# First block: x loaded in two halves, late half turned behind the first products, second weight chunk in quarters, rotation tables and memory rows moved

## The reference

```python
h = rms_norm(x, norm_mix)
aq, ak, av, iq, ik, iw, bq, bk, bv = _split(h @ w_in, AB_SIZES)      # AB_WIDTH 2472
aq = partial_rope(rms_norm(aq.reshape(B, S, DSA_HEADS, HEAD_DIM), a_q_norm), positions)
ak = partial_rope(rms_norm(ak.reshape(B, S, 1, HEAD_DIM), a_k_norm), positions)[:, :, 0]
iq = partial_rope(iq.reshape(B, S, DSA_IDX_HEADS, DSA_IDX_DIM), positions)
o_a = dsa_attention(aq, ak, av, iq, ik, iw)       # top 64 keys by an index score
bq, bk = ...
o_b = moba_attention(bq, bk, bv)
x = x + concatenate([o_a, o_b]) @ w_out
```

## Time and profile before

| | us |
|---|---|
| median of 3 runs | 1660.42 |
| lowest, highest | 1660.26, 1661.79 |
| span of the profiled execution, from the first to the last instruction | 1659.6 |
| TensorE busy | 1619.1 (98%) |
| VectorE busy | 1096.3 (66%) |
| ScalarE busy | 891.3 (54%) |
| POOL busy | 421.5 (25%) |

### The profile page before, as it was taken

How to read it: one execution, slowest core, us unless ns; L and a number is a source line. 1 busy time by engine, 2 the same in 40 slices (tenths; PEclk the granted TensorE clock), 3 DMA queues, 4 the chain that set the end, 5 groups by cost and what they waited for, 6 DMA issues and landing times. The chain is left out here.

```text
span 1659.6 us, 26949 instructions
## 1 busy us (share of the span) xinstructions
PE 1619.1 (98%) x10929; PEld 1462.8 (88%) x10929; DVE 1096.3 (66%) x1546; ACT 891.3 (54%) x1401; POOL 421.5 (25%) x460
## 2 busy tenths in 40 slices
PE   8999999999999999999999999999999999999999
PEld 7767899987887889998889998999888999999997
DVE  6875665645576665655577768777646876867763
ACT  6465554434455555443456746566445684756652
POOL 2500100002341120000147802244204690214430
PEclk9999999999999999999999999999999999999999
DMA  7523376556330236665555444766556444376652
GB/s 278 174 77 101 103 205 194 185 197 213 99 135 27 77 102 172 185 186 193 174 195 164 147 133 147 189 185 190 181 154 220 159 153 130 131 204 187 190 179 76
DMA packets 287067, 265.30 MB, mean 160 GB/s; under 512 B 12256, under 2 KB 247520, under 8 KB 286944
## 3 DMA queue, kind: packets, MB, share of 16 engines
q1 hardware_dynamic: 286944, 263.59, 50.8%
HBM read 262.52 MB, written 1.05 MB: 159 GB/s over the span
## 5 line engine op out<-in xcount | busy, mean ns | idle before, releaser
L144 DVE TENSOR_TENSOR w_lo<-w_raw,w_hi 128x2048 fp32r<-128x2048 f32 (+2 forms) x244 | 565.8, 2321 | 288.6 <-ACT w_hi L143 283.6
L143 ACT ACTIVATE w_hi<-w_raw 128x2048 fp32r<-128x2048 f32 (+2 forms) x244 | 462.9, 1902 | 214.6 <-PE bank L529 125.5
L1873 PE MATMUL bank<-h_hi,w_hi 128*128 128x256 f32 x1984 | 565.5, 285 | 4.7 <-issue 1.2
L1874 PE MATMUL bank<-h_lo,w_hi 128*128 128x256 f32 x1984 | 561.3, 283 | 0.0
L1875 PE MATMUL bank<-h_hi,w_lo 128*128 128x256 f32 x1984 | 561.2, 283 | 0.0
L1873 PEld LDWEIGHTS bank<-h_hi,w_hi 128*128 128x128 f32 x1984 | 380.5, 192 | 8.2 <-issue 7.5
L1874 PEld LDWEIGHTS bank<-h_lo,w_hi 128*128 128x128 f32 x1984 | 380.7, 192 | 0.1
L1875 PEld LDWEIGHTS bank<-h_hi,w_lo 128*128 128x128 f32 x1984 | 380.6, 192 | 0.0
L456 PE MATMUL bank<-w_hi,h_hi 128*128 128x512 f32 (+1 forms) x288 | 113.4, 394 | 5.4 <-DVE w_lo L144 3.3
L2953 POOL TENSOR_TENSOR cffn_hidden<-cffn_conv 128x256 f32<-128x256 f32 x44 | 73.7, 1675 | 155.5 <-ACT cffn_conv L2984 155.5
L457 PE MATMUL bank<-w_lo,h_hi 128*128 128x512 f32 (+1 forms) x288 | 111.9, 388 | 0.0
(11 more groups left out here) (447 smaller groups left out, 2858.0 us busy)
## 6 DMA issues: line engine op xcount, KB each, us to landing
w_raw<-in_w_in SPq DMA_DIRECT2D x48, 1024.0 KB, 5.0
w_raw<-in_ffn_w_in SPq DMA_DIRECT2D x88, 512.0 KB, 5.0
w_raw<-in_w_up SPq DMA_DIRECT2D x88, 512.0 KB, 5.2
w_raw<-in_ffn_w_out SPq DMA_DIRECT2D x22, 1024.0 KB, 4.9
w_raw<-in_w_down SPq DMA_DIRECT2D x22, 1024.0 KB, 5.0
w_raw<-in_nsa_w_in SPq DMA_DIRECT2D x10, 1024.0 KB, 5.2
w_raw<-in_mem_w_kv SPq DMA_DIRECT2D x8, 1024.0 KB, 5.1
w_raw<-in_w_branch SPq DMA_DIRECT2D x8, 1024.0 KB, 5.1
```

Source lines behind the costliest of these rows:

```text
L143: return act.activation(hi, raw, ACT.Copy)
L144: return dve.tensor_tensor(self.lo[:, cut_slot, 0:k * n], raw, hi.bitcast(F32), ALU.subtract)
L1873: pe.matmul(out, h, hi[:, f, :], start=(f == 0), stop=False)
L1874: pe.matmul(out, h, lo[:, f, :], start=False, stop=False)
```

## The change

x comes in two DMAs of 512 columns each, with the gains, the positions and chunk 0's first half between them. TensorE turns the first half of the features before the first product, and the second half (`turn_late`) inside block 0, behind the six products of feature 0. Chunk 1 goes through `FirstChunk` as well: loaded in two halves, rounded and cut in four tiles. On ScalarE it is now rounded behind the squares and the table activations. On VectorE the 17 table instructions stand behind tile 1 of chunk 0. POOL fills the tables' inputs before it waits for the squares. The memory rows are loaded before chunk 3 and turned behind chunk 2, at (1, 0). The head gains are loaded last.

```diff
 class FirstChunk:
-    def __init__(self, k, chunk):
+    def __init__(self, k, chunk, c):
...
-        self.landed = [self.w.early_in[0], s("first_landed")]
-        self.rounded, self.cut = s("first_rounded"), s("first_cut")
+        self.landed = [self.w.early_in[c], s(f"first_landed{c}")]
+        self.rounded, self.cut = s(f"first_rounded{c}"), s(f"first_cut{c}")
...
 Project.pe
-                if c or self.tiles is None:
+                if c not in self.tiles:
                     w.wait_cut(pe, c)
...
+                    if j == 0 and ahead is not None:
+                        ahead(pe, f)
                     if j == 0:
                         self.features.wait_feature(pe, f)
-                    if c == 0 and self.tiles is not None:
-                        self.tiles.wait_cut(pe, k)
+                    if c in self.tiles:
+                        self.tiles[c].wait_cut(pe, k)
...
 block.sync
-                sp.dma_start(k.x[:, :, :], a["x"].rearrange("(t p) d -> p t d", p=P)).then_inc(x_in, 16)
+                x = a["x"].rearrange("(t p) d -> p t d", p=P)
+                sp.dma_start(k.x[:, :, 0:D // 2], x[:, :, 0:D // 2]).then_inc(x_in, 16)
                 sp.dma_start(k.gains_1[:, :], a["cols_1"]).then_inc(cols_in, 16)
+                rope_tables.load(sp)
+                first[0].load(sp, 0)
+                sp.dma_start(k.x[:, :, D // 2:D], x[:, :, D // 2:D]).then_inc(x_in_late, 16)
+                first[0].load(sp, 1)
                 for part in range(2):
-                    first.load(sp, part)
-                for c in range(1, w.EARLY):
-                    w.load(sp, w.chunks[c], w.raw_slot(c), w.early_in[c])
+                    first[1].load(sp, part)
+                w.load(sp, w.chunks[2], w.raw_slot(2), w.early_in[2])
+                mem.load(sp)
+                w.load(sp, w.chunks[3], w.raw_slot(3), w.early_in[3])
                 sp.dma_start(gain[:, :], row_bcast(a["rows"], 256)).then_inc(gains_in, 16)
-                rope_tables.load(sp)
-                mem.load(sp)
...
 block.gpsimd
+                rope_tables.pool(pool)
                 rows.factors(pool, 4)
-                rope_tables.pool(pool)
...
 block.scalar
-                for i in range(3):
+                for i in range(2):
                     rows.round(act, range(2 * i, 2 * i + 2))
-                    first.round(act, i)
-                first.round(act, 3)
+                    first[0].round(act, i)
+                rows.round(act, range(4, 6))
+                first[0].round(act, 2)
                 rows.round(act, range(6, KD))
-                w.round_to(act, 1)
+                first[0].round(act, 3)
                 for t in range(T):
                     for part in range(2):
+                        if part == 1:
+                            act.wait_ge(x_in_late, 16)
                         rows.square(act, t, part)
+                rope_tables.act(act)
+                for i in range(4):
+                    first[1].round(act, i)
                 w.round_to(act, 2)
-                rope_tables.act(act)
...
 block.vector
-                for i in range(3):
+                for i in range(2):
                     rows.cut(dve, range(2 * i, 2 * i + 2))
-                    first.split(dve, i)
-                first.split(dve, 3)
+                    first[0].split(dve, i)
+                rope_tables.dve(dve)
+                rows.cut(dve, range(4, 6))
+                first[0].split(dve, 2)
                 rows.cut(dve, range(6, KD))
-                w.cut_to(dve, 1)
-                rope_tables.dve(dve)
+                first[0].split(dve, 3)
+                for i in range(4):
+                    first[1].split(dve, i)
+                w.cut_to(dve, 2)
...
 block.tensor
                 pe.wait_ge(x_in, 16)
-                rows.turn_all(pe)
+                for t in range(T):
+                    rows.turn(pe, t, 0)
+
+                def turn_late(pe, f):
+                    if f == 1:
+                        pe.wait_ge(x_in_late, 16)
+                        for t in range(T):
+                            rows.turn(pe, t, 1)
...
-                    if (j, part) == (0, 1):
+                    if (j, part) == (1, 0):
                         mem.turn(pe)
...
-                project.pe(pe, index)
+                project.pe(pe, index, turn_late)
```

More of the change, by code:

```diff
@@ L207 @@
 class FirstChunk:
-    def __init__(self, k, chunk):
+    def __init__(self, k, chunk, c):
         s, self.w, (self.rows, self.n, sources) = k.sems, k.weights, chunk
-        self.source = sources[0][1]
-        self.landed = [self.w.early_in[0], s("first_landed")]
-        self.rounded, self.cut = s("first_rounded"), s("first_cut")
+        self.c, self.source = c, sources[0][1]
+        self.landed = [self.w.early_in[c], s(f"first_landed{c}")]
+        self.rounded, self.cut = s(f"first_rounded{c}"), s(f"first_cut{c}")
     def load(self, sp, part):
@@ L219, in load @@
         tiles = slice(half * part, half * part + half)
-        dst = self.w.raw[:, self.w.raw_slot(0), 0:self.rows * self.n].rearrange("p (k n) -> p k n", k=self.rows)
+        dst = self.w.raw[:, self.w.raw_slot(self.c), 0:self.rows * self.n].rearrange("p (k n) -> p k n", k=self.rows)
         sp.dma_start(dst[:, tiles, :], self.source[:, tiles, :]).then_inc(self.landed[part], 16)
@@ L224, in parts @@
         columns = slice(self.n * i, self.n * i + self.n)
-        raw, hi, lo = self.w.raw_slot(0), self.w.cut_slot(0), self.w.cut_slot(0)
+        raw, hi, lo = self.w.raw_slot(self.c), self.w.cut_slot(self.c), self.w.cut_slot(self.c)
         return self.w.raw[:, raw, columns], self.w.hi[:, hi, columns], self.w.lo[:, lo, columns]
@@ L233, in round @@
         if last:
-            self.w.act_next = 1
+            self.w.act_next = self.c + 1
     def split(self, dve, i):
@@ L238, in split @@
         last = i == self.rows - 1
-        dve.wait_ge(self.w.rounded if last else self.rounded, 1 if last else i + 1)
+        dve.wait_ge(self.w.rounded if last else self.rounded, self.c + 1 if last else i + 1)
         dve.tensor_tensor(lo, raw, hi.bitcast(F32), ALU.subtract).then_inc(self.w.cut if last else self.cut, 1)
         if last:
-            self.w.dve_next = 1
+            self.w.dve_next = self.c + 1
     def wait_cut(self, pe, i):
         if i == self.rows - 1:
-            self.w.wait_cut(pe, 0)
+            self.w.wait_cut(pe, self.c)
         else:
@@ L430, in __init__ @@
         self.hi, self.lo = features.hi, features.lo
-        self.short, self.tiles = short, tiles
+        self.short, self.tiles = short, tiles or {}
         self.copied_a, self.copied_d = k.sems(name + "_copied_a"), k.sems(name + "_copied_d")
@@ L434, in __init__, with pe @@
         self.last = [first + (0 if n == 256 else 1) for first, (_, _, n) in zip(self.first, blocks)]
-    def pe(self, pe, after=None):
+    def pe(self, pe, after=None, ahead=None):
         w = self.k.weights
@@ L1125, in block_dsa_moba @@
         blocks = [(c, c, min(512, AB_W - c)) for c in (512, 0, 1024, 1536, 2048)]
-        first = FirstChunk(k, ab_first(a)[0])
+        first = [FirstChunk(k, ab_first(a)[c], c) for c in range(2)]
+        x_in_late = s("x_in_late")
         x_in, cols_in, filled = s("x_in"), s("cols_in"), s("filled")
-        project = Project(k, "proj", a["ab_w_in"], AB_W, blocks, rows, proj, tiles=first)
+        project = Project(k, "proj", a["ab_w_in"], AB_W, blocks, rows, proj, tiles=dict(enumerate(first)))
         mem = MemoryRows(k, a, 0, feat[:, 0:8, :].rearrange("p (t a) b -> p t (a b)", t=T),
```

## The result

| | before | after |
|---|---|---|
| median of the comparison, us | 1661.08 | 1668.03 |
| lowest to highest | 1660.26 to 1661.79 | 1667.58 to 1668.43 |
| span of the profiled execution | 1659.6 | 1666.5 |

The ratio is 1.0042 with a 95% interval of 1.0028 to 1.0056: the changed kernel is 7 us slower. The forecast was 1664.3 with a range to 1667.2. It had added its +3.9 to 1660.42, the median of three runs; with the fourth run the median before is 1661.08, so 0.66 us of the distance to the forecast lies in where it started.

The account below looks back on a forecast made before the run. The prediction took TensorE, busy 98% of the span, as the bound. At chunk 5, +4.9 at chunk 4 less 0.95 at the index scores made +3.9 us, added to a median of 1660.42: 1664.3, range 1661.6 to 1667.2.

Parts of the forecast that it names:

- +3.9: Summed delay at chunk 5's start in us: +4.9 at chunk 4 less 0.95 at the index scores, kept to the end.
- The early half: Weight loads of x's turn: an earlier landing half gains 0.15 us, bounds 0 and 0.19.
- The table steps: VectorE's 17 rotation-table steps run from 11.3 to 15.5, ahead of features 4 and 5, with only 2.1 us to spare.
- The rests before feature 2 and chunk 1: TensorE rests from 14.0 to 17.1 before feature 2 and from 19.8 to 20.5 before chunk 1.
- chunk 4's cut: On VectorE, starts 6.9 us after the first memory feature, at 39.5; chunk 4 starts at 41.95 instead of 37.07.
- the rest at the index scores: TensorE's 0.9 us wait for a VectorE copy goes, since TensorE ends chunk 4 after that copy: -0.95 us.
- the prediction's part on the clock: Falls to 1.2 GHz behind two new early rests of 2.7 and 3.1 us, left out of the sum.
- rival 1: Clock falls in one new rest: 1664.3 + 0.9 to 1.75, say 1665.7; both or longer: up to 1667.5; chance 0.28.
- the fall there: Later block, before the change: granted clock at 0.50 for 3.4 us after a short rest, costing 1.7 us of work.
- the first rest: TensorE rests 2.7 us before feature 0, 7.4 to 10.1; a clock fall behind it costs up to 1.75 us.
- The rest of 2.3 in front of chunk 4: Listed among the signs to see in the profile after: TensorE rests 2.3 us before chunk 4.
- the late half of x: Fourth data transfer of SP's queue, landed by 9.0 at the latest and wanted at 11.5, so it costs nothing.

Follow-up runs that it names:

- Experiment 4: Changed kernel with chunks 1 and 2 rounded on ScalarE ahead of the squares and table activations: 1666.09 us, ratio 1.003.
- 8: Kernel before with only the memory rows' turn moved behind chunk 2: 1666.86 us against 1660.89, ratio 1.003.
- 10: Changed kernel with the memory rows turned behind chunk 1 again and chunks 1 and 2 rounded ahead of the squares: 1662.47 us, ratio 1.001.
- experiment 3: Changed kernel plus unread transposes in two rests, 18 behind the early turn and 16 ahead of chunk 4: 1665.98 us, ratio 1.0029.
- Experiments 2: Changed kernel with all 16 transposes of x ahead of the first product again, x still in two halves: 1665.64 us, ratio 1.0026.
- 12: Changed kernel with all x transposes ahead of the first product and the positions' DMA issued behind chunk 1: 1668.19 us, ratio 1.0043.
- 9: Changed kernel with four rests filled by unread transposes (18 behind the early turn, 22 before feature 2, 8 before chunk 1, 18 before chunk 4): 1665.55 us.
- 5: Kernel before with POOL's fills of the rotation tables' inputs moved ahead of the wait for the squares: 1660.93 us against 1660.89, ratio 1.0002.
- experiment 1: Changed kernel with the memory rows turned behind chunk 1 again: 1665.16 us, ratio 1.0026.

## Why the prediction was wrong

**Right: the mechanism and its direction, step by step.** The early half won 0.01 to 0.1 us (0.15 forecast). The table steps stood at 11.3 to 15.2 in front of features 4 and 5 (11.3 to 15.5). The rests before feature 2 and chunk 1 came, though with other lengths (1.23 and 2.49 us, 3.1 and 0.7 forecast), chunk 4's cut waited 6.95 us behind the memory features (6.9), the rest at the index scores went. Experiment 4 shows ScalarE's order alone, 8 the memory turn alone, 10 both undone together.

**The step that failed** is in the prediction's part on the clock: "I leave it out of the sum, because no row of this stretch shows a fall, and keep it as a rival." The clock fell twice, and rival 1, the right one, was bounded at 1667.5, under the 1668.03 that came, and left partly outside the range, which ended at 1667.2. The term that stood at nothing is measured: chunk 5 starts at 51.78 with the two falls and at 48.28 with these rests filled (experiment 3). Of these 3.5 us 0.6 is the earlier start of feature 0, which the fillers can't have made, so 2.9 are the clock's. In the medians it is 2.0 (1668.03 and 1665.98), or 2.4 when each is taken against the kernel before measured with it (7.0 and 4.5).

The reason for leaving it out was weak, and so was what the forecast drew from the earlier trace rows. It took the fall there as support for a fall behind a long rest. TensorE's rows of that place, before, show a rest of only 0.52 us, behind 32 products of 32 columns:

```profile
467.39 3.66 PE L2323 MATMUL bank<-nsa_cmp_kf,nsa_feat_q 128*128 128x32 f32 x32
471.57 0.70 PE L890 MATMUL bank<-w_hi,h_hi 128*128 128x512 f32 x1 [0.52 <-DVE h_lo L303]
```

So these rows said nothing of long rests. Behind its warm-up the kernel before has no rest over 1.72 us at all, and none of its rows could show what one of 2.4 to 2.8 does.

**Where the falls were.** I priced them for the first rest (2.7 forecast, 2.59 measured; "up to 1.75": chunk 2 came 2.0 later than forecast, at 27.99 against 26.0, and with this rest filled at 26.09) and for the one before feature 2. The second never grew to 3.1 us: since the slow late turn pushed feature 1 to 14.0, TensorE rested 1.23 and kept its clock. In experiment 3, where the late turn was fast, this rest was 2.77 and the clock fell behind it. The rest of 2.3 in front of chunk 4, which the forecast names and sizes, was not on the list at all, and there nothing behind it absorbs a slow chunk: from chunk 4 to chunk 5 it is 7.90 us after and 6.30 in experiment 3, so 1.6 us in full.

**A bound that was wrong without cost.** I had the late half of x landed by 9.0 "at the latest", counting it as the fourth transfer of the queue; it was the fifth that SP issued, and landed at 2.7 + 6.9 = 9.6. It was wanted at 12.4. Experiments 2 and 12 show what it costs where it is wanted sooner, and that it lands about 1.3 us later for the positions' DMA ahead of it. Why it took 5.8 us to land even then is not settled.

**Left open.** Between the forecast and experiments 3 and 9, which keep the clock up in the rests that were filled, lie 1.3 to 1.7 us of the time. More than half of it is the starting point: against the kernel before measured with them both lose 4.5 us, where the forecast had 3.9, so 0.6 is left. The 7.0 us of the changed kernel are then 3.9 that were forecast, 2.4 of the clock and 0.6 that stay open. At chunk 5 they agree with the forecast within 0.1 and 0.7 us. The stretch between the first products of two groups of L1873 (199.69 to 628.43 before), which holds nothing of the change, takes 428.7 us in the profile before, 428.2 after and 429.8 in the profiles of experiments 3, 5 and 9, with the clock's low stretches at different places in it. So what is left need not be the change's; how much of it is was not measured.

## What to carry to other kernels

Price a rest of the bound engine twice: once as its length, once as what the clock may do in the work behind it, at every rest that the forecast names, and ask whether another wait follows soon enough to swallow the slow stretch. Moving work behind a later step costs what the next consumer's whole chain costs (here 6.9 us of rounding, squaring and rounding in one queue), not the work's own length. When a wait is removed, look up when every other input of the same instruction is there: the DMA of 1 KB had been late all along behind POOL's fills.

## What the runs showed of the hardware that I had not expected

- TensorE's clock can fall after rests shorter than I thought. In the first 60 us of the fourteen profiles (before, after and the twelve experiments) there are 14 rests of 2.4 to 2.8 us between two groups of TensorE's work; behind 10 of them the granted clock was at 0.50 for about 3.4 us, behind 4 it was not. Behind the rests of up to 1.7 in this stretch it never was; in a later block it was behind one of 0.52, as the two rows above show. The same rest of 2.49 before chunk 1 was survived in the changed kernel and not in experiment 1, so from one profile to the next a fall may move.
- Work that nobody reads made a kernel 2 us faster (experiment 3), because it kept the clock up: with all four rests filled by transposes (experiment 9) the granted clock is 1.00 all through the first 50 us.
- The positions' DMA carries 1 KB, and issuing it behind chunk 1 instead of ahead of chunk 0 made the second half of x land 1.3 us sooner (9.34 and 8.05), some 0.5 of it since its own DMA is issued that much earlier.
